# Sums over partitions in the second norm, the last norm and four heads: split fp32r matmuls in place of fp32 ones

## What is computed

```
def rms_norm(x, g):
    xf = x.astype(jnp.float32)
    y = xf * lax.rsqrt(jnp.mean(xf * xf, axis=-1, keepdims=True) + EPS)
    return (y * g.astype(jnp.float32)).astype(x.dtype)
...
    x = x + 0.5 * swiglu(rms_norm(x, n_f1), wg1, wu1, wd1)
    h = rms_norm(x, n_mix) @ w_in
...
    o = o * lax.rsqrt(jnp.mean(o * o, axis=-1, keepdims=True) + EPS)
    o = o * gla_norm.astype(jnp.float32).reshape(H_C, DV_C)
    y = o.reshape(bsz, t, D_C).astype(r.dtype) * jax.nn.silu(r)
...
    x = x + jnp.concatenate([y_a, y_b, y_c], axis=-1) @ w_o
    x = x + 0.5 * swiglu(rms_norm(x, n_f2), wg2, wu2, wd2)
    gate = jax.nn.sigmoid(rms_norm(x, n_ple) @ w_ple_gate)
    x = x + gate * (p.astype(x.dtype) @ w_ple_proj)
```

## Time and profile before

| | |
|---|---|
| median of three runs | 1957.09 us (1955.86 to 1959.09) |
| the profiled execution | 1957.27 us, its span 1955.4 us |
| TensorE matmul busy | 1928.9 us, 99% |
| TensorE weight load busy | 1907.5 us, 98% |
| VectorE busy | 1295.5 us, 66% |
| ScalarE busy | 759.2 us, 39% |
| GpSimd busy | 93.9 us, 5% |
| granted TensorE clock | 0.998 of full |

### The profile page before, as it was taken

One profiled execution on the slowest core, in us unless ns is written; L12 is line 12 of the kernel. 1 busy time (PEld: TensorE's weight loads), 2 busy tenths in 40 slices (PEclk: granted clock), 3 DMA queues, 4 the chain that ended last, 5 costly groups with the idle time before them and its releaser, 6 DMA issues.

```text
span 1955.4 us, 36344 instructions
## 1 busy us (share of the span) xinstructions
PE 1928.9 (99%) x14762; PEld 1907.5 (98%) x14762; DVE 1295.5 (66%) x1819; ACT 759.2 (39%) x1069; POOL 93.9 (5%) x71
## 2 busy tenths in 40 slices
PE   8999999999999999999999999999999999999998
PEld 8899999999999999999999989999999999999998
DVE  6966767667886874244446587676676686868634
ACT  7533333334342454021164363333333352433534
POOL 0000000000000002010040120000000000000121
PEclk9999999999999999999999999999999999999999
DMA  6232232325551532111132032322223354441202
GB/s 199 83 104 82 82 134 90 103 82 204 182 199 39 166 114 76 44 34 32 32 128 66 22 110 83 123 100 97 88 82 115 109 199 174 174 158 47 83 27 89
DMA packets 142701, 202.84 MB, mean 104 GB/s; under 512 B 5752, under 2 KB 116048, under 8 KB 139152
## 3 DMA queue, kind: packets, MB, share of 16 engines
q1 hardware_dynamic: 142608, 201.51, 30.5%
HBM read 146.58 MB, written 54.91 MB: 103 GB/s over the span
## 4 chain that ended last, share of the span: by engine, by line
PE 87%; DVE 7%; ACT 2%; issue 2%; DMA 1%; SPq 0%; DVEq 0%; ACTq 0%
PE ps L2681 62%; PE ps L2619 21%; DVE wr_lo L1714 1%; DVE x L1961 1%; PE ps L2735 1%; DVE xl L2408 1%; PE ps L2644 1%; DMA wpair<-in_w_ffn_gate 0%; PE ps L2952 0%; DVE op_lo L1854 0%; PE ps L2972 0%; PE ps L2847 0%; PE ps L2978 0%; PE ps L2909 0%; ACT xh L1060 0%
## 5 line engine op out<-in xcount | busy, mean ns | idle before, releaser
L2681 PE MATMUL ps<-op_hi,wr_hi 128*128 128x264 f32 x3640 | 743.9, 285 | 12.4 <-ACT sr L1154 3.3
L2681 PE MATMUL ps<-op_lo,wr_hi 128*128 128x264 f32 x3640 | 742.8, 285 | 0.0
L2681 PE MATMUL ps<-op_hi,wr_lo 128*128 128x264 f32 x3640 | 742.1, 285 | 0.0
L2681 PEld LDWEIGHTS ps<-op_hi,wr_hi 128*128 128x128 f32 x3640 | 566.6, 188 | 17.8 <-issue 7.4
L2681 PEld LDWEIGHTS ps<-op_lo,wr_hi 128*128 128x128 f32 x3640 | 565.1, 188 | 0.0
L2681 PEld LDWEIGHTS ps<-op_hi,wr_lo 128*128 128x128 f32 x3640 | 564.8, 189 | 0.0
L1110 ACT ACTIVATE wr_hi<-wr_raw 128x512 fp32r<-128x512 f32 (+1 forms) x268 | 164.7, 619 | 375.9 <-DVE wr_raw L1724 146.3
L2619 PE MATMUL ps<-xh,wh 128*128 128x352 f32 x888 | 197.7, 330 | 1.0 <-DVE tg L2527 0.5
L1714 DVE TENSOR_TENSOR wr_lo<-wr_raw,wr_hi 128x512 fp32r<-128x512 f32 (+1 forms) x268 | 174.3, 675 | 25.2 <-ACT wr_hi L1110 14.6
L2619 PE MATMUL ps<-xh,wl 128*128 128x352 f32 x888 | 190.0, 322 | 0.0
L1110 ACT ACTIVATE wr_hi<-wpair 128x512 fp32r<-128x512 f32 (+1 forms) x201 | 122.9, 615 | 149.9 <-PE ps L2681 136.7
(11 more groups left out here) (308 smaller groups left out, 1686.3 us busy)
## 6 DMA issues: line engine op xcount, KB each, us to landing
h_ops<-hq SPq DMA_DIRECT2D x22, 1848.0 KB, 7.0
op_raw<-h_ops SPq DMA_DIRECT2D x28, 1056.0 KB, 8.1
wpair<-in_w_ffn_up SPq DMA_DIRECT2D x22, 1024.0 KB, 5.3
wpair<-in_w_ffn_gate SPq DMA_DIRECT2D x21, 1024.0 KB, 9.0
wpair<-in_w_ffn_down SPq DMA_DIRECT2D x16, 1024.0 KB, 8.6
wst<-in_w_in SPq DMA_DIRECT2D x22, 512.0 KB, 3.8
op_raw<-h_ops SPq DMA_DIRECT2D x14, 792.0 KB, 5.0
wpair<-in_w_ffn_down SPq DMA_DIRECT2D x8, 768.0 KB, 5.1
```

What stands on the lines that cost most here:

```text
L2681: last = pe.matmul(ps[:, out + h, 0:TQ], w_[idx][:, m, :], x_[:, n, h * TQ:h * TQ + TQ], start=idx in (0, 1, 3) and m == 0 and w_ is wr_hi ...
```

## The change

The sums of norms 1 and 3 and of heads 1 to 4 are made of fp32r matmuls: the squares are split into a high and a low part, the matrix of ones is copied to fp32r, and each fp32 matmul becomes two fp32r ones that accumulate in PSUM. Norm 2 and the samples of the heads stay as they are. For the norms, ScalarE makes the high part (`sum_high`) and VectorE the low one, in the place of the sum (`sum_low`). For a head, ScalarE squares into `osq` as before, waits for its own square, and copies it to `or_hi[n % 2]`, which lies where `or_tile[n % 2]` lies; VectorE puts the low part into `osq`. Norm 1 is summed one block later (after k = 2). ScalarE squares head 3 after the three exponentials and the split for `u_r[3]`, and heads 3 and 4 wait for `o_norm(0)` and `o_norm(1)`; their sums move from after k = 0 and 5 of `u_r[2]` to after k = 2 and 7.

```diff
@@
+        ones_r = at("ones_r", [P, P], F32R, rows.manual_sbuf_range[0])
+        osq_lo = at("osq_lo", [P, T], F32R, offset=osq.manual_sbuf_range[0])[:, 0:seq]
+        sum_hi = {1: at("sum_hi1", [P, T], F32R, OPS + 5 * SLOT + HOLE),
+                  3: at("sum_hi3", [P, T], F32R, OPS + 2 * SLOT + HOLE)}
+        sum_lo = {1: at("sum_lo1", [P, T], F32R, OPS + 4 * SLOT + HOLE),
+                  3: at("sum_lo3", [P, T], F32R, OPS + SLOT + HOLE)}
+        or_hi = [at(f"or_hi{b}", [P, T], F32R, RING + b * T * 4)[:, 0:seq] for b in range(2)]
@@ ScalarE
+            def sum_high(norm):
+                act.wait_ge(sq_added, (KT - 1) * norm)
+                act.activation(sum_hi[norm][:], sum_of[norm][:], ACT.Copy).then_inc(sum_hi_set, 1)
@@
             split_hi(u_va[1])
+            act.wait_ge(cols_set, 2)
+            act.activation(ones_r[:], ones[:], ACT.Copy)
+            sum_high(1)
             norm_log(1)
@@ def o_square(n)
                 if n > 1:
                     act.wait_ge(or_full, n)
+                if n > 2:
+                    act.wait_ge(o_normed, n - 2)
                 act.activation(osq[:, 0:seq], mix[:, V_ + n - 1, 0:seq], ACT.Square, scale=float(dv) ** -0.5
-                               ).then_inc(osq_set, 1)
+                               ).then_inc(o_raw, 1)
+                act.wait_ge(o_raw, n)
+                act.activation(or_hi[n % 2], osq[:, 0:seq], ACT.Copy).then_inc(osq_set, 1)
@@
             o_log(2)
-            o_square(3)
             for n in range(3):
                 o_scale(n)
             split_hi(u_r[3])
+            o_square(3)
             o_log(3)
@@
                     p_hi_round(1)
+                    sum_high(3)
@@ VectorE
+            def sum_low(norm):
+                dve.wait_ge(sum_hi_set, {1: 1, 3: 2}[norm])
+                dve.tensor_tensor(sum_lo[norm][:], sum_of[norm][:], sum_hi[norm][:].bitcast(F32), ALU.subtract
+                                  ).then_inc(sq_lo_set, 1)
@@
             split_lo(u_va[1])
+            sum_low(1)
@@
+            def o_low(n):
+                dve.wait_ge(osq_set, n + 1)
+                dve.tensor_tensor(osq_lo, osq[:, 0:seq], or_hi[n % 2].bitcast(F32), ALU.subtract
+                                  ).then_inc(sq_lo_set, 1)
+
             scale_r(0)
+            o_low(1)
             conv(0)
             split_lo(u_r[2])
+            o_low(2)
             conv(1)
             o_norm_samples()
             o_norm(0)
             o_norm(1)
+            o_low(3)
             split_lo(u_r[3])
             scale_r(1)
+            o_low(4)
             o_norm(2)
@@
                     p_lo_round(1)
+                    sum_low(3)
@@ TensorE
+            def split_means(high, low, bank):
+                for b in range(2):
+                    cs = slice(b * seq // 2, (b + 1) * seq // 2)
+                    pe.matmul(ps[:, bank + b, :], ones_r[:], high[:, cs], start=True, stop=False)
+                    last = pe.matmul(ps[:, bank + b, :], ones_r[:], low[:, cs], start=False, stop=True)
+                return last
@@ def norm_means(norm)
+                if norm != 2:
+                    pe.wait_ge(sq_lo_set, {1: 1, 3: heads + 2}[norm])
+                    pe.matmul(r_sample_of(norm), ones_r[:], sum_hi[norm][:, seq:T], start=True, stop=False)
+                    pe.matmul(r_sample_of(norm), ones_r[:], sum_lo[norm][:, seq:T], start=False, stop=True)
+                    split_means(sum_hi[norm], sum_lo[norm], r_banks(norm)).then_inc(r_full, 1)
+                    return
@@
-            project(u_va[0], SET_B, hooks={1: lambda: norm_means(1)})
+            project(u_va[0], SET_B, hooks={2: lambda: norm_means(1)})
@@ def o_means(n)
                     pe.wait_ge(o_log_set, n)
-                    last = means(osq, 6)
+                    pe.wait_ge(sq_lo_set, n + 1)
+                    last = split_means(or_hi[n % 2], osq_lo, 6)
@@
-                       {0: lambda: o_means(3), 5: lambda: o_means(4)}, {}]
+                       {2: lambda: o_means(3), 7: lambda: o_means(4)}, {}]
```

More of the change, by code:

```diff
@@ L361, in hybrid_trunk @@
         log_set = sem("log_set")
+        sum_hi_set = sem("sum_hi_set")
+        sq_lo_set = sem("sq_lo_set")
         o_log_set = sem("o_log_set")
@@ L438, in hybrid_trunk @@
         yc_last = sem("yc_last")
+        o_raw = sem("o_raw")
         osq_set = sem("osq_set")
```

## The result

| | before | changed |
|---|---|---|
| median of ten runs | 1956.63 us (1953.08 to 1959.09) | 1964.03 us (1959.24 to 1967.65) |
| profiled execution, its span | 1957.27, 1955.4 | 1963.71, 1961.9 |

What follows compares the result with a forecast made beforehand. TensorE, busy for 99% of 1955.4 us, was taken to bound the kernel. Heads +6.5, second norm -0.77 and last norm -0.7 gave +5.0 on 1957.27, 1962.3 us (1962.2 against the median); range 1958.8 to 1965.3.

Steps and rivals of the forecast that it cites:

- Price of a sum: On TensorE, four fp32r matmuls of 512 columns take 0.94 us instead of 1.71, saving 0.77 per sum.
- Head 2: At head 2's sum, GpSimd's hold delays VectorE's low half to 1003.2; TensorE, there at 1002.55, waits 0.65 us.
- Head 3: At head 3's sum, the low half, behind o_norm(0) and holds, is ready at 1017.35; TensorE waits 6.0 us.
- Head 4 and the chain: Head 4's logarithm starts 6.5 us later; the slackless chain behind it moves TensorE's restart from 1045.06 to 1051.5.
- Second norm: The second norm's sum saves 0.77 us, its new wait costed at 0, upper end 0.2; later loads cost nothing.
- Last norm: The last norm's sum gains 0.7 us, with a wait of at most 0.1; the gate's chain moves along.
- Rival 1: Shorter holds at head 3: low half at 1015.9 or 1015.2, total +3.5 or +2.9, about 1960.5 us; chance 0.25.
- rival 2: Heads' waits covered, only the chain's slack counts: heads gain 0.2, norms 1.5, total 1955.6 us; chance 0.05.
- rival 3: Full gain, with slack in the chain behind head 4: six sums give 4.6 us, total 1952.7; chance 0.03.
- rival 5: Sums don't get shorter in fp32r: 3.1 us more than forecast, 1965.4; chance 0.12 together with rival 4.
- Rival 4: New collisions after 1045 or costlier norm waits add some 2 us, 1964.5; chance 0.12 together with rival 5.

Runs made afterwards that it cites:

- own_place: Changed kernel with the heads' high half in free words of its own and head 3's square before the exponentials again; 1959.07 us.
- before_hook7: Kernel before, nothing split, with head 4's sum made after the eighth block of its projection instead of the sixth; 1959.31 us.
- busy_early: Changed kernel with twenty extra fp32r matmuls, result overwritten, ahead of all of head 3's waits on TensorE; 1960.83 us.
- heads: Only the heads' part of the change, norms in fp32 as in the kernel before; 1966.21 us, before 1956.84.
- norms_keep: Kernel before with only the norms' sums split, and VectorE scaling the v_a tile before splitting the first q tile's weights; 1955.55 us against 1955.16.
- busy: Changed kernel with twenty extra fp32r matmuls ahead of head 3's wait for its low half, but behind the wait for the square's copy; 1966.08 us.
- hook5: Changed kernel with head 4's sum moved back from after the eighth block to after the sixth; 1962.50 us.

## Why the prediction was right, and where it was off

Forecast: 1962.2 us, slower, by waits at heads 2 and 3 and by the later sum of head 4. Measured: 1964.03, inside the range by 1.3 us at its upper end. Both waits and the later sum were there; the clock after the wait and the wait at gate_z(0) were in no term of the sum.

- **Price of a sum.** 0.94 us and a saving of 0.77 were predicted; the four matmuls of head 4 start 0.23 us apart, 0.92 for the four. Right. The Trainium skill's 0.216 us ("TensorE: Matmul & The Clock Gate", Back-to-back issue gap) is 6% below what is measured here; the row of 352 columns was the better guide.
- **Head 2.** Predicted wait 0.65, measured 0.65.
- **Head 3.** Predicted start of the sum 1017.4 on the clock of before. Measured 1015.63, with the samples' sum at 992.59 in place of 994.11, which is 1017.15 on the same clock. The wait was to be 6.0 and was 5.41 idle; `own_place` shows what makes it. The holds were shown for the convolution and the samples too, as the Trainium skill's "GPSIMD Engine Reference" (Key points) has it for instructions with two SBUF inputs; they were smaller at the convolution (0.48 us in place of 0.85).
- **Head 4 and the chain.** Shown by `before_hook7` without any splitting (2.89 us in B) and by the restart's wait of 2.47. Right in mechanism. **The step that was mis-sized** is the projection between the two sums, "1017.4 + 0.94 + 5 x 1.45 = 1025.6": it assumed the full clock. From head 3's to head 4's sum it took 9.63 us in place of 8.2, because TensorE's clock had fallen to one half in the wait; with the wait filled (`busy_early`) it took 8.24. So the heads cost 7.6 us in this profile, not 6.5, and in the profile of `heads`, with 10.7 between the sums, 8.7.
- **Second norm.** "Gain 0.77" was wrong in what follows: the sum did become 0.8 us shorter and its new wait was none, but 0.55 us were lost again at gate_z(0), which started 0.47 us late and whose first three matmuls took 0.08 longer. I had costed the loads behind the sum at nothing, as feeding work due after 740; VectorE's scaling of the v_a tile stands in its queue behind a split that waits for such a load, and TensorE arrived before it. ScalarE's copy of that load began 17.64 us after the projection's start before and 18.29 after: it is the load that moved. `norms_keep` shows that the scaling's place behind it makes the wait.
- **Last norm.** Predicted 0.7: from the samples' columns of the sum (1830.98 before, 1836.96 after) to the gate's restart are 7.18 us before and 6.46 after, 0.72 less. Right.

Together: -0.78 + 0.55 + 7.61 - 0.72 = +6.7 us, against +5.0 predicted and +8 (6.1 to 10.0) measured. That the rest lies in longer slow stretches of the clock in other executions is my reading. Two things on record lean that way. Of the changed kernel's ten executions the four with a mean granted clock of 0.994 or 0.995 took 1964.36 to 1967.65 us, the six with 0.996 or 0.997 took 1959.24 to 1964.62. And in the profile of `heads` the clock cost 2.5 us at head 3 and 1.3 after the output projection's wait, 3.8 together, where the changed kernel's profile lost 1.4. Where the other executions lost their time wasn't measured.

Rival 1 (shorter holds) fell with a low half that was ready at 1017.0 on the clock of before, near the forecast's 1017.35 and not at 1015.9, and rival 2 (the waits are covered) with the wait of 5.41; rival 3 fell with `before_hook7`, rival 5 with the 0.23 us. Rival 4 (more delay, 1964.5) is nearest in number, and the measured +8 lies above the +4 to +6 that the forecast was given. Of what it names, the norms' delay came true with 0.55 us; the larger part is the clock, which no rival had. That the range held it is due in part to a room at the top that was reasoned from other causes.

## What to carry to other kernels

A cheaper instruction on the busiest engine pays only where the work that prepares its inputs doesn't make them late: follow the new inputs through the queues of the engines that make them, and look for where the new buffer lies, since here the shared place and the order that goes with it cost 5.8 us, while the four shorter sums save 3.1. A sum that heads a chain without slack can't be moved later to cover its inputs; take something out of the chain instead. And price a new wait of several microseconds on TensorE with the slow stretch after it.

## What the runs showed that I had not expected

After 5.41 us without work TensorE's matmuls of 512 columns took 0.43 us each, and they and the blocks after them 1.4 us more in all; the granted clock was 0.50, that is 1.2 GHz. After 3.00 us (`busy`) it was 0.54 from 1016 to 1018, and after 0.65 it stayed at 1.00. After the 2.47 or 2.48 us at the output projection it went both ways: it fell to 0.50 in two of seven profiles, `heads` (1.3 us more for eighteen matmuls) and `busy` (1.5), and stayed at 1.00 in the other five. So the same wait can cost or not, and one profile doesn't tell which. The time until the full clock was back differed: the loss was 1.4 us in the changed kernel's profile, 2.4 in `hook5`, 2.5 in `heads`. The Trainium skill ("TensorE: Matmul & The Clock Gate", Back-to-back issue gap) has N/1.2 ns for this state, 0.427 us for 512 columns, which the trace bears out.

GpSimd and VectorE took turns instruction by instruction: VectorE's low half of head 2 got in between GpSimd's product and its 32 columns, which then took 1.22 us in place of 0.26.
